# Latent attention handed to TensorE head by head, its V product made for two pairs at a time, and every squares sum split in two rounded parts

## The reference

```python
def mla_layer(h, w_dqkv, q_lora_norm, w_uq, kv_lora_norm, w_ukv, ...):
    cq, ckv, k_rope = jnp.split(h @ w_dqkv, [384, 640], axis=-1)
    q = (rms_norm(cq, q_lora_norm) @ w_uq).reshape(bsz, seqlen, 16, 64 + 32)
    kv = (rms_norm(ckv, kv_lora_norm) @ w_ukv).reshape(bsz, seqlen, 16, 64 + 64)
    q_nope, q_rope = jnp.split(q, [64], axis=-1)
    k_nope, v = jnp.split(kv, [64], axis=-1)
    q_nope, k_nope = rms_norm(q_nope, ...), rms_norm(k_nope, ...)
    q_rope, k_rope = apply_rope(rms_norm(...), cos, sin)
    s = (q_nope @ k_nope + q_rope @ k_rope) * scale, causal
    o = softmax(s) @ v
    return o @ w_o
```

## Time and profile before

| | us |
|---|---|
| median of 3 runs | 2898.31 (2897.52 to 2899.02) |
| the profiled execution | 2898.93 |
| its span | 2897.1 |
| PE busy in it | 2864.6 (99%) |
| POOL busy | 1848.9 (64%) |
| DVE busy | 1301.5 (45%) |
| ACT busy | 565.8 (20%) |

### The profile page before, as it was taken

One profiled execution on the slowest core, in us unless ns is written; L12 is line 12 of the kernel. 1 busy time (PEld: TensorE's weight loads), 2 busy tenths in 40 slices (PEclk: granted clock), 3 DMA queues, 4 the chain that ended last, 5 costly groups with the idle time before them and its releaser, 6 DMA issues.

```text
span 2897.1 us, 36332 instructions
## 1 busy us (share of the span) xinstructions
PE 2864.6 (99%) x13536; PEld 2326.3 (80%) x13536; DVE 1301.5 (45%) x1506; ACT 565.8 (20%) x821; POOL 1848.9 (64%) x1822
## 2 busy tenths in 40 slices
PE   9999999999989999999999999999999999999998
PEld 6778888888867778888888888788888777788887
DVE  5765545414355654414444223444244455543241
ACT  4550221000124541000111101210001445300000
POOL 5557548777752238777775565677777544677775
PEclk9999999999999999999999999999999999999999
DMA  4112213232220102222232222222322111222322
GB/s 152 61 60 88 74 57 111 80 108 100 84 85 28 38 29 87 92 103 102 80 125 85 74 94 81 73 100 80 105 95 91 69 63 54 72 95 84 106 92 89
DMA packets 38583, 242.35 MB, mean 84 GB/s; under 512 B 4288, under 2 KB 4672, under 8 KB 16608
## 3 DMA queue, kind: packets, MB, share of 16 engines
q1 hardware_dynamic: 37296, 237.19, 23.5%
q10 hardware_dynamic: 1200, 3.96, 0.4%
HBM read 239.04 MB, written 2.10 MB: 83 GB/s over the span
## 4 chain that ended last, share of the span: by engine, by line
PE 94%; DVE 3%; ACT 1%; DVEq 1%; issue 0%; ACTq 0%; DMA 0%; SPq 0%
PE ps L402 67%; PE ps L435 13%; PE ps L1345 1%; PE ps L1161 1%; PE ps L1301 1%; PE ps L1180 1%; PE ps L1382 1%; PE ps L1362 1%; PE ps L1395 1%; PE ps L1377 1%; PE ps L1291 1%; DVEq L2262 0%; DVEq L1857 0%; PE ps L1053 0%; DVE scr L2235 0%
## 5 line engine op out<-in xcount | busy, mean ns | idle before, releaser
L716 POOL CAST w_hi<-raw 128x512 fp32r<-128x512 f32 (+1 forms) x909 | 677.5, 761 | 1030.7 <-PE ps L402 836.7
L704 POOL TENSOR_TENSOR w_lo<-raw,w_hi 128x512 fp32r<-128x512 f32 (+1 forms) x909 | 1220.0, 1354 | 0.1
L402 PE MATMUL ps<-h_hi,w_hi 128*128 128x512 f32 x1904 | 751.7, 395 | 3.3 <-DVE h_lo L1868 3.0
L402 PE MATMUL ps<-h_hi,w_lo 128*128 128x512 f32 x1904 | 742.0, 390 | 0.0
L402 PE MATMUL ps<-h_lo,w_hi 128*128 128x512 f32 x1904 | 741.5, 389 | 0.0
L402 PEld LDWEIGHTS ps<-h_hi,w_hi 128*128 128x128 f32 x1904 | 357.8, 188 | 80.8 <-issue 5.3
L402 PEld LDWEIGHTS ps<-h_hi,w_lo 128*128 128x128 f32 x1904 | 357.6, 188 | 75.7
L402 PEld LDWEIGHTS ps<-h_lo,w_hi 128*128 128x128 f32 x1904 | 357.9, 188 | 75.1 <-issue 2.9
L402 PE MATMUL ps<-a_hi,w_hi 128*128 128x512 f32 x816 | 319.7, 392 | 2.2 <-issue 1.4
L402 PE MATMUL ps<-a_hi,w_lo 128*128 128x512 f32 x816 | 318.3, 390 | 0.0
L402 PE MATMUL ps<-a_lo,w_hi 128*128 128x512 f32 x816 | 318.1, 390 | 0.0
(11 more groups left out here) (319 smaller groups left out, 3614.2 us busy)
## 6 DMA issues: line engine op xcount, KB each, us to landing
...
raw<-weights SPq DMA_DIRECT2D x8, 512.0 KB, 3.5
...
x_out<-x SPq DMA_DIRECT2D x1, 2048.0 KB, 6.3
...
```

What stands on the lines that cost most here:

```text
L402: mm = pe.matmul(out_ap, a, b, start=(i == 0 and not begun), stop=(i == n - 1 and ended))
L704: pool.tensor_tensor(w_lo[:, slot, parts[j]], raw[:, slot, parts[j]], w_hi[:, slot, parts[j]].bitcast(F32), ALU.subtract).then_inc(s_split ...
L716: pool.tensor_copy(w_hi[:, slot, piece], raw[:, slot, piece]).then_inc(s_hi[j], 1)
```

## The change

The program differs in these points.

1. The norms' and retention's sums of squares are split by DVE into a rounded part and a rest, and multiplied by rounded ones in two rounded matmuls, in place of one float32 matmul. That is seven norms and four retention heads. DVE gets a cast, a subtraction and a copy of the ones for each norm.
2. GLA's last head: six matmuls of the output projection's second column pair are moved ahead of `mean`.
3. Latent attention's V is projected for two pairs at once (256 columns streamed), and only in every second pair; the weight chunks of a pair are now 1536 and 1024 wide in turn, in place of 1280. The even product is spread over two places, ahead of `k_mean` and between the two heads' `weighted`. ACT copies it out in four pieces.
4. `q_means` is taken apart: head 0's mean goes ahead of `scores_turned` of head 0, head 1's right behind it, and `proj_k` goes ahead of `scores_turned` of head 1.
5. ACT takes the inverse root of each head on its own, and DVE makes q and k head by head: q of head 0, the turned products of head 1, k of head 0, which raises `s_mq` for head 0, then k of head 1 and the last two operations of head 1's q, which raise it for head 1. TensorE waits for each head on its own.
6. In the prologue of latent attention, five set-up copies go from DVE to ACT, DVE writes k's rotated part for one buffer in place of two (ACT copies the other), and the order of DVE and ACT around the first pair is changed.
7. The result is stored tile by tile, eight DMAs of 256 KB, each as soon as its tile is final.

Its core:

```diff
-STAGE_WIDTHS = {"ssd": [384] + [2048] * 15, "gla": [2048] * 15, "mla": [2048] * 3 + [1280] * 8 + [2048] * 4,
+STAGE_WIDTHS = {"ssd": [384] + [2048] * 15, "gla": [2048] * 15, "mla": [2048] * 3 + [1536, 1024] * 4 + [2048] * 4,
...
-            sp.wait_ge(s_res, 8 * n_res + 2)
-            sp.dma_start(out, x[:, :, :]).then_inc(s_out, 16)
-            sp.wait_ge(s_out, 16)
+            for k in range(KD):
+                sp.wait_ge(s_res, 8 * (n_res - 1) + k + 3)
+                sp.dma_start(out[:, k, :], x[:, k, :]).then_inc(s_out, 16)
+            sp.wait_ge(s_out, 16 * KD)
...
-                pe.matmul(ps[:, norm_bank(name), :], ones, norm_sq[:, 0, :], start=True, stop=True).then_inc(s_mean, 1)
+                pe.matmul(ps[:, norm_bank(name), :], n_ones, n_hi, start=True, stop=False)
+                pe.matmul(ps[:, norm_bank(name), :], n_ones, n_lo, start=False, stop=True).then_inc(s_mean, 1)
...
                 residual_begun("gla", (4, 5))
+                residual_begun("gla", (0,), 1)
                 mean(hd)
-                residual_begun("gla", range(6), 1)
+                residual_begun("gla", range(1, 6), 1)
...
+                def proj_v(w, part):
+                    if part == 0:
+                        pe.wait_ge(s_mln, 2 * w + 2)
+                    else:
+                        pe.wait_ge(s_mr, 3 * w + 3)
+                    for tb in (2 * part, 2 * part + 1):
                         s = slice(tb * P, (tb + 1) * P)
-                        mm = product(pe, ps[:, 7, s], [(h_hi[:, k, s], h_lo[:, k, s], *kv_weights(par, k, P))
-                                                       for k in range(2)])
-                    mm.then_inc(s_used, 1)
-
-                def q_means(w):
-                    for e in range(2):
-                        pe.wait_ge(s_msl, 2 * w + e + 1)
-                        pe.matmul(ps[:, 6 + e, :], m_blkq, m_sqh[:, e, :], start=True, stop=False)
-                        pe.matmul(ps[:, 6 + e, :], m_blkq, m_sql[:, e, :], start=False, stop=True).then_inc(s_mm, 1)
+                        mm = product(pe, ps[:, 7 - part, (tb % 2) * 256:(tb % 2) * 256 + 256],
+                                     [(h_hi[:, k, s], h_lo[:, k, s], *kv_weights(0, k, P, 2 * P)) for k in range(2)])
+                    mm.then_inc(s_used if part else s_mvp, 1)
+
+                def q_mean(w, e):
+                    pe.wait_ge(s_msl, 2 * w + e + 1)
+                    pe.matmul(ps[:, 6 + e, :], m_blkq, m_sqh[:, e, :], start=True, stop=False)
+                    pe.matmul(ps[:, 6 + e, :], m_blkq, m_sql[:, e, :], start=False, stop=True).then_inc(s_mm, 1)
...
                 def pair(u, par, first, ahead):
                     nxt = 1 - par
-                    pe.wait_ge(s_mq, u + 1)
                     for e in range(2):
+                        pe.wait_ge(s_mq, 2 * u + e + 1)
                         scores(u, par, e, first)
 
-                    pe.wait_ge(s_mv, u + 1)
+                    pe.wait_ge(s_mv, u + 1 if par else u + 2)
                     if ahead:
                         proj_q(u + 1, nxt, 0)
                         proj_q(u + 1, nxt, 1)
@@ -1208,19 +1218,24 @@
                         residual_begun("mla", (0, 1))
                     max_turned(u, 0)
                     max_turned(u, 1)
-                    if not ahead:
+                    if ahead:
+                        q_mean(u + 1, 0)
+                    else:
                         residual_begun("mla", (2,))
                     scores_turned(u, par, 0)
                     if ahead:
-                        q_means(u + 1)
+                        q_mean(u + 1, 1)
+                        proj_k(u + 1, nxt)
                     else:
                         residual_begun("mla", (3,))
                     scores_turned(u, par, 1)
                     if ahead:
-                        proj_k(u + 1, nxt)
-                        proj_v(u + 1, nxt)
+                        if par:
+                            proj_v(u + 1, 0)
                         k_mean(u + 1)
                     weighted(u, par, 0)
+                    if ahead and par:
+                        proj_v(u + 1, 1)
                     weighted(u, par, 1)
                     if not ahead:
                         residual_begun("mla", (4, 5, 6))
@@ -1230,11 +1245,15 @@
                 proj_q(0, 0, 0)
                 latent_sum(0, (3, 4))
                 proj_q(0, 0, 1)
-                q_means(0)
+                pe.wait_ge(s_mcr, 3)
+                q_mean(0, 0)
+                q_mean(0, 1)
                 pe.wait_ge(s_mh, 5)
                 proj_k(0, 0)
                 k_mean(0)
                 proj_v(0, 0)
+                proj_v(0, 1)
+                pe.wait_ge(s_mkrope, 2)
...
+                act.activation(m_ident, phase_const("mla", "mla_ident"), ACT.Copy)
+                act.activation(m_mask, phase_const("mla", "mla_mask"), ACT.Copy)
+                act.activation(m_blkq, const("blkq"), ACT.Copy)
+                for e in range(2):
+                    act.activation(h_hi[:, 6 + e, :], x[:, e, :], ACT.Copy, scale=0.0)
...
+                def v_copied(w, n, slot, part):
+                    if slot == 0 and part:
+                        wait_used(c0 + 3 + w)
+                    elif slot == 0:
+                        act.wait_ge(s_mvp, n + 1)
+                    ins = act.activation(
+                        m_v[:, slot, 2 * part:2 * part + 2, :].rearrange("p t (x n) -> p t x n", x=3)[:, :, 0:3:2, :],
+                        ps[:, 7 - part, :].rearrange("p (t w e n) -> p t w e n", t=2, w=2, e=2)[:, :, slot, :, :], ACT.Copy)
+                    if part:
+                        ins.then_inc(s_mv, 1)
 
...
+                def pair(u, par, ahead, n):
                     if ahead:
                         q_squared(u + 1)
+                        q_rstd(u + 1, 0)
                     exps(u, 0)
                     if ahead:
-                        q_rstd(u + 1)
+                        q_rstd(u + 1, 1)
+                        k_squared(u + 1, not par, n)
                     exps(u, 1)
                     if ahead:
-                        k_squared(u + 1)
-                        v_copied(u + 1, 1 - par, first)
                         k_rstd(u + 1)
+                    if ahead and par:
+                        v_copied(u + 1, n, 0, 0)
                     sums_inverted(u, 0)
+                    if ahead and par:
+                        v_copied(u + 1, n, 0, 1)
                     sums_inverted(u, 1)
-
+                    if ahead and par:
+                        for part in range(2):
+                            v_copied(u + 2, n, 1, part)
...
-                for w in range(2):
-                    rope_in_k(w)
+                                      ALU.add).then_inc(s_mkrope, 1)
+
+                rope_in_k(0)
...
+                def heads_ready(w, par):
+                    q_turned(w, 0)
+                    q_ready(par, 0)
+                    q_turned(w, 1)
+                    k_ready(w, par, 0).then_inc(s_mq, 1)
+                    k_ready(w, par, 1)
+                    q_ready(par, 1).then_inc(s_mq, 1)
...
                 if k == KD - 1:
-                    ins.then_inc(s_acc, 1)
+                    dve.tensor_copy(n_ones, ones)
+                    split(n_hi, n_lo, norm_sq[:, 0, :]).then_inc(s_acc, 1)
...
                 latent_total(3, 0, 1.0 / 256)
-                wait_used(c0 + 2)
-                dve.tensor_copy(m_ident, phase_const("mla", "mla_ident"))
-                dve.tensor_copy(m_mask, phase_const("mla", "mla_mask"))
-                dve.tensor_copy(m_blkq, const("blkq"))
-                for e in range(2):
-                    dve.tensor_scalar(h_hi[:, 6 + e, :], cos, 0.0, None, ALU.mult)
                 q_square_low(0, 0)
                 dve.wait_ge(s_mcr, 3)
+                latent_normed(3)
                 q_square_low(0, 1)
-                for k in (3, 4):
-                    latent_normed(k)
-                q_normed(0)
-                q_ready(0)
-                k_ready(0, 0)
+                latent_normed(4)
+                heads_ready(0, 0)
```

123 lines of the change are left out of this document (60 added, 63 removed).

## The result

The changed kernel takes 2875.03 us, the median of 4 runs (2872.49 to 2876.61); the kernel before took 2898.43 beside it (2897.52 to 2899.02). The ratio is 0.9916 with a 95% interval of 0.9901 to 0.9932: 23.4 us faster. Forecast were 2871 in a range of 2864 to 2880, so the direction and the range held, and the gain is 3.7 smaller than the 27.1 of the sum.

What follows compares the result with a forecast made beforehand. PE, busy 2864.6 of 2897.1 us, was taken as the bound. Gains of 4.6 + 11.8 + 6.0 + 1.4 + 3.3 = 27.1 from the median 2898.31 gave 2871, range 2864 to 2880.

Steps and rivals of the forecast that it cites:

- The squares sums: Norms and retention: two rounded matmuls replace each float32 sum, 0.42 on PE at eleven sums; 4.6, ends 3.5 and 4.6.
- the cover of 3.7: Norms: margin between DVE's last addition and PE reaching the sum; 2.1 of added DVE work leaves 1.6.
- V for two pairs: Latent attention's pairs: three V products of 2.89 replace seven of 2.62, gaining 9.6 on PE.
- the waits in the pairs: Latent attention: 2.4 and seven times 0.2 gained, 1.6 lost to a new border wait; net 2.2, ends -1.5 and 4.5.
- does nothing by itself: Latent attention's pairs: splitting q and k by heads alone gains nothing, as PE was held only 0.2 at a border.
- The prologue: Latent attention's start: k's product 4.4 earlier, pair 0 5.0 earlier, about 1.0 less low clock after; together 6.0.
- rival B: Latent attention's prologue: the clock never falls, adding 4.2; 2865 to 2867; chance 0.16.
- the 1.6 for ACT: Latent attention's prologue, if the clock does not fall: ACT's part of the 6.8 from k's product to pair 0.
- GLA's mean: GLA's last head: six matmuls moved into PE's 1.6 wait for the split sum; 1.4 gained, at worst 1.0.
- The store: Kernel's end: the last 256 KB DMA takes 3.0 where one 2048 KB DMA took 6.3; gain 3.3, ends 2.8 and 5.5.
- Rival C: Latent attention: clock stays low as long as before, DVE 0.9 late at all seven borders; gain 18.4, 2880; chance 0.22.
- D: Latent attention's pairs: DVE becomes the bound, pairs take 29.9, 12 slower, 2910; chance 0.02.

Runs made afterwards that it cites:

- The kernel with V behind k's mean: Against the kernel with V projected in every pair, rest as changed (2893.52 us): V's 24 matmuls moved behind k's mean; 2882.69 us, ratio 0.9943.
- The kernel with the late release: Against the changed kernel: in pairs without V, the weight chunk goes to POOL by the last weighted sum's third matmul, not k's product; 2868.28 us.
- the kernel with the early read: Against the changed kernel: DVE reads head 0's bank between k's rows and head 1's last two sums of q; 2873.31 us, ratio 0.9909.
- filled waits: Against the changed kernel: 22 dummy matmuls, into a bank nobody reads, put in the waits of latent attention's prologue; 2874.64 us.

## Why the prediction was right, and where it was off

- **What bounds.** Right: PE, 99% before and after, and 20.7 of its busy us gone.
- **The squares sums, 4.6 forecast, 2.8 measured**, below the 3.5 that was the lower end. 0.42 to 0.45 for each where PE is the bound, as computed, eight times. Missed was what the split costs beside POOL. From the end of DVE's last addition to the end of its subtraction it takes 3.4 to 3.7 at the feed-forward layers' norms, not the 2.1 of the sum (the copy of the ones alone takes 1.31), so the cover of 3.7, read from one norm and taken for all, was used up: the first feed-forward layer's sum came just in time, and PE waited 0.38 for the last one's. At the first POOL's split was held up in turn, and PE waited for that (0.49). Stick-breaking's norm gives nothing since PE already waited for DVE behind it (1.4), and DVE's cast and subtraction made it 1.8 (L1352).
- **V for two pairs, 9.6, and the waits in the pairs, 2.2.** This is the step that was furthest off, in size. Together 9.7 came, not 11.8. The prediction named the new wait "of 0 to 0.9, in four pairs" and took 1.6 in sum; it was three times 0.85 and once 3.1, 5.65. Without the wait, 13.4 was forecast and 15.35 came (12.8 and 2.55 for the waits of the first seven pairs), 0.3 better in each pair: those without V took 22.6 where 22.9 was forecast. The kernel with V behind k's mean tells why: the border did hold PE for 0.2, but the wait shown as 0.34 cost 0.50, and the first matmuls after the border took 0.1 longer. The timing of DVE was put together from durations that DVE has with POOL at rest or in the old place, and the release of the 1024 wide chunk, which the change moves from the end of V to `proj_k`, was not followed to POOL and back to DVE. The kernel with the late release shows that without it there is no wait; the kernel with the early read shows that the order of DVE's rows had its part.
- **That V's gain is "sure as long as nothing else then ends last".** The condition was the point. Taken alone it is not only lost but reversed, since V's matmuls hid ACT and DVE. The statement that splitting by heads "does nothing by itself" was wrong too: with V ahead of k's mean it costs 3.4 over seven pairs, and with V behind it it gives 5.0.
- **The prologue, 6.0 forecast, 7.0 measured.** Near in size, wrong in its share, and so in part by luck: 2.0 from the moved work, where 4.4 was forecast, and the rest from the order. Both waits were as forecast or shorter (1.92 and 0.4 for squares, 1.1 for the latent). The clock fell again, for a shorter time than before: 10 us from 854.1, and no longer into pair 0, where it had been 20 us from 856.7. V's matmuls of 256 columns were no dearer there than the 128 wide ones, as taken: 0.213 each at the lower clock in both kernels. The rival B, no fall, did not occur; filled waits show what it would have given, 2.8 and not 4.2. (Of its terms the 1.6 for ACT is 1.7 by the numbers beside it.)
- **GLA's mean, 1.4 forecast, 1.4 measured.** The six matmuls filled the wait but for 0.2.
- **The store, 3.3 forecast, 4.3 measured.** The last 256 KB took 2.4 from issue to the end, not 3.0: nearer to the 2.6 that stood beside it by the Trainium skill ("DMA: Bandwidth & Descriptors", section "Anatomy of one DMA — SWDGE (gpsimd) path") than to the line through two sizes. That section is on DMAs that GpSimd issues, and SP issues this one.
- **Rival C** was right on the mechanism at one point (POOL's split beside DVE at the border), and its size of 0.9 was right for three of the four; **D** did not come near: DVE is busy 47%.

Open: why the clock falls near 193 us in some executions and not in others, and so which 1.5 to 4 us of the medians above belong to chance; and why the wait of pair 7 is 3.1 where the others are 0.85. There DVE's work beside POOL is slowed for longer, and the chunk that POOL splits is one of the output projection's, 2048 wide:

```profile
1030.46 2.62 DVE L2237 TENSOR_TENSOR scr<-scr 16x512 f32<-16x512 f32 x2
1033.10 2.67 DVE L2283 SCALAR_TENSOR_TENSOR scr<-scr,par 64x512 f32<-64x512 f32 x2
1035.78 1.66 DVE L2277 TENSOR_TENSOR scr<-scr 128x512 f32<-128x512 f32 x1
1037.52 1.60 DVE L2278 TENSOR_TENSOR scr<-scr 48x512 f32<-48x512 f32 x1
1039.21 1.47 DVE L2312 TENSOR_TENSOR scr<-ps,scr 64x512 f32<-64x512 f32 x2
```

```profile
1035.19 3.38 POOL L710 TENSOR_TENSOR w_lo<-raw,w_hi 128x512 fp32r<-128x512 f32 x2
```

Each of DVE's operations up to 1039.12 takes 0.6 to 1.0 us more than alone. That fits, and the late release took this wait away too; that the chunk's width sets the size was not tried by itself.
